# Turning x1's first half inside the attention loop, with its terms in DRAM, and attention and mixing in one block

## The chip, the cores and the metric

The kernel runs on one core of a Trainium2 chip. The metric is the device time of one execution in microseconds (us), taken as the median of several runs; the kernel before needs 1972.02 us (three runs, 1969.37 to 1972.77). The names of the engines are those of the profile: PE (matmuls; PEld is its weight load), DVE (vector), ACT (scalar activation), POOL (GpSimd), and SP, which in this kernel issues every DMA, in the order in which its program is written.

## The reference

Two residual layers run over x (2048 rows by 1024 columns, float32). The first is gated linear attention, the second a causal pooling mixer. What is computed, cut to what matters here:

```python
# layer 0: gated linear attention, chunks of 64 rows
q, k, v, g, lr = split(x @ gla_w_in)
o = o_intra + qe @ S_prev                       # o_intra: masked scores @ v
o = o * rsqrt(mean(o**2) + 1e-6) * norm_w * silu(g)
x1 = layernorm(4**0.25 * x + o @ gla_w_out)
# layer 1: pooling mixer
u, z = split(x1 @ pool_w_in)                    # 2048 columns each
p = causal_window_means(u) - u                  # windows of 2, 4, 8, 16 rows
m = (p @ w_grp + b_grp) * scale
out = layernorm(4**0.25 * x1 + (m * silu(z)) @ pool_w_out)
```

## The kernel before

Every large float32 product is split: an operand is written as a high part (a rounded copy, made by ACT) and a low part (the operand minus the high part, made by DVE), and `split_product` (L198) issues three matmuls, high by high, low by high, high by low. The large products are further done by a seven-product scheme on 2 by 2 blocks (`PRODUCTS`, `ORDER` = 1, 5, 6, 2, 7, 3, 4), so that each "step" of the projection and mixing stages is seven products of four k slices each, and the operand x has seven terms: blocks 1, 2 and 3 are quarters of x itself, terms 5, 6, 7 and 4 are sums and differences of quarters.

The program runs in four stages, one block each: `prepare` (fuses pooling weights with the group weights), `project` (x @ gla_w_in), `attend_and_norm` (attention, output projection and layer norm, giving x1), and `pool_mix_and_out` (the mixing stage and the final projection). At the end of a block every engine waits for all others.

**Attention** takes 16 tiles of 128 rows. In step t, PE does the scores and the state update of tile t, then the first half of the output projection of tile t - 2 (`y_half`, with the two matmuls of `mean` for tile t - 1 in the middle), then `outputs` of tile t, then the second half of the projection. ACT and DVE make the high and low parts, the gate, and the norm of tile t - 3; SP loads q, k, k2, kn, v for tile t + 2, g, and x, and stores x1's tile t - 3. Steps 4 to 13 are a hardware loop, the others are written out.

**Mixing** has 32 steps (16 pairs of weight columns, over x1's first half and then its second half), and 16 output steps. x1 is needed transposed. Its second half is turned on the way, during steps 2 to 9, in eight "chunks": `load_stage_rows` brings rows of x1 back from DRAM, PE transposes them (`turn_stage`), ACT copies them out of PSUM (`copy_stage`), POOL makes the four sums (`stage_terms`), and SP stores seven pieces into the DRAM scratch `x_terms` (`store_stage`). When the operand set changes (after step 15, `LAST_OF_EPOCH`), the terms are loaded from there; ACT and DVE split them (`turn_hi`, `turn_lo`), except that in the first step after a change the products at positions 4 and 5 (`NATIVE`; terms 7 and 3) run unsplit on the raw term (L2250), so that their splitting can come later. The first half has no such step before it: at the start of the mixing block it is turned at once. `turn_first` transposes 4 times 2 row tiles, `first_parts` and `first_terms` (ACT), `first_term` (POOL) and `first_sums`, `first_terms_lo` (DVE) make all terms with their high and low parts, and only then can step 0's first product start.

## Time and profile before

| what | us |
|---|---|
| median of the runs | 1972.02 (1969.37 to 1972.77) |
| the profiled execution, whole | 1964.6 |
| its span, first to last instruction | 1962.9 |
| PE busy | 1861.6 (95%) |
| DVE busy | 1398.3 (71%) |
| ACT busy | 852.5 (43%) |
| POOL busy | 598.2 (30%) |

The profile is of one execution. A row of a timeline gives the start, the duration, the engine, the line of the kernel and the tiles written and read; what stands in brackets is how long the engine was idle before it and what ended that. The recorded duration of a matmul is longer than its share of a pipelined row: the distance from one start to the next is what a matmul costs there. The slices of the page show PE at 9 tenths nearly everywhere, with two dips, one near 640 us (the border between projection and attention) and one near 970 us (the border between attention and mixing).

### The profile page before, as it was taken

To read this page: it belongs to the slowest core of one execution; us is meant where nothing else is said; L and a number is where in the kernel's file an instruction comes from. 1 tells how busy PE (TensorE), PEld (TensorE's weight loads), DVE (VectorE), ACT (ScalarE), POOL (GpSimd) and SP (SyncE) were. 2 spreads that over 40 slices of the span, in tenths; PEclk is the share of its full clock that TensorE was granted. 3 is DMA by queue.
4 is the path that set the end of the run, shared out by engine and by line. 5 is a ranking of instruction groups with operands and counts; after the bars stand their busy time and mean duration, and the time that the engine had idled before them with its cause. 6 is when DMAs were issued, how large, how long until landed. Compare 5 with 4: busy or idle time off the path is not lost.

```text
span 1962.9 us, 24653 instructions
## 1 busy us (share of the span) xinstructions
PE 1861.6 (95%) x8688; PEld 1535.0 (78%) x8688; DVE 1398.3 (71%) x1769; ACT 852.5 (43%) x1323; POOL 598.2 (30%) x380
## 2 busy tenths in 40 slices
PE   8989999999999699999679999999999998999997
PEld 7878887886788588888558888887888786887786
DVE  3454555778667678787666788768899967546997
ACT  4554445657555434333444444344333344224221
POOL 1322231332221000000145665405566532323330
PEclk9999999999999799999879999999999999999999
DMA  8967572557365645443413544242546326556442
GB/s 286 321 200 266 195 248 97 152 141 247 90 171 179 239 145 188 171 162 138 171 43 116 170 150 144 98 172 75 178 170 221 140 93 215 208 192 257 161 151 97
DMA packets 259725, 336.43 MB, mean 171 GB/s; under 512 B 18208, under 2 KB 187936, under 8 KB 255904
## 3 DMA queue, kind: packets, MB, share of 16 engines
q1 hardware_dynamic: 259616, 335.02, 50.9%
q8 instruction: 63, 1.03, 0.2%
q14 instruction: 46, 0.38, 0.1%
HBM read 218.58 MB, written 116.39 MB: 171 GB/s over the span
## 4 chain that ended last, share of the span: by engine, by line
PE 38%; DVE 7%; issue 4%; ACT 1%; POOL 0%; DVEq 0%; ACTq 0%; POOLq 0%
PE banks L200 13%; PE banks L202 12%; PE banks L201 12%; DVE m_w_lo L2520 2%; DVE m_x_lo L2534 1%; DVE m_win_a L2550 1%; ACT m_x_hi L2310 0%; DVE m_res L2633 0%; DVE m_win_b L2550 0%; DVE m_x_lo L2512 0%; PE banks L2203 0%; PE banks L2250 0%; DVE m_win_b L2566 0%; DVE m_res L2617 0%; DVE m_x_lo L2494 0%
## 5 line engine op out<-in xcount | busy, mean ns | idle before, releaser
L200 PE MATMUL banks<-m_x_hi,m_w_hi 128*128 128x512 f32 x1320 | 517.7, 392 | 12.6 <-DVE m_z L2596 6.6
L201 PE MATMUL banks<-m_x_lo,m_w_hi 128*128 128x512 f32 x1320 | 515.1, 390 | 0.0
L202 PE MATMUL banks<-m_x_hi,m_w_lo 128*128 128x512 f32 x1320 | 514.9, 390 | 0.0
L200 PEld LDWEIGHTS banks<-m_x_hi,m_w_hi 128*128 128x128 f32 x1320 | 248.8, 188 | 68.7 <-DVE m_w_lo L2520 10.6
L202 PEld LDWEIGHTS banks<-m_x_hi,m_w_lo 128*128 128x128 f32 x1320 | 248.7, 188 | 52.1
L201 PEld LDWEIGHTS banks<-m_x_lo,m_w_hi 128*128 128x128 f32 x1320 | 248.6, 188 | 51.8 <-issue 0.7
L200 PE MATMUL banks<-b_hi,h_w_hi 128*128 128x512 f32 x656 | 257.9, 393 | 6.1 <-issue 4.5
L202 PE MATMUL banks<-b_hi,h_w_lo 128*128 128x512 f32 x656 | 256.3, 391 | 0.0
L201 PE MATMUL banks<-b_lo,h_w_hi 128*128 128x512 f32 x656 | 256.0, 390 | 0.0
L2298 ACT ACTIVATE m_w_hi<-m_s 128x512 fp32r<-128x512 f32 x184 | 115.5, 629 | 186.2 <-PE banks L202 166.0
L2436 POOL TENSOR_TENSOR m_s<-pair_raw 128x512 f32<-128x512 f32 x24 | 46.7, 1945 | 469.0 <-POOLq L1512 365.1
L2520 DVE TENSOR_TENSOR m_w_lo<-m_s,m_w_hi 128x512 fp32r<-128x512 f32 x184 | 157.5, 857 | 32.3 <-ACT m_w_hi L2298 30.2
L200 PEld LDWEIGHTS banks<-b_hi,h_w_hi 128*128 128x128 f32 x656 | 123.6, 188 | 33.8 <-issue 8.6
L202 PEld LDWEIGHTS banks<-b_hi,h_w_lo 128*128 128x128 f32 x656 | 123.5, 188 | 26.0
L201 PEld LDWEIGHTS banks<-b_lo,h_w_hi 128*128 128x128 f32 x656 | 123.7, 189 | 25.4
L1224 DVE TENSOR_TENSOR h_w_lo<-h_s,h_w_hi 128x512 fp32r<-128x512 f32 x94 | 70.3, 753 | 48.9 <-ACT h_w_hi L954 48.3
L200 PE MATMUL banks<-a_w_hi,a_o_hi 128*128 128x512 f32 x256 | 101.5, 397 | 2.3 <-DVE a_res L1748 1.7
L201 PE MATMUL banks<-a_w_lo,a_o_hi 128*128 128x512 f32 x256 | 100.1, 391 | 0.0
L202 PE MATMUL banks<-a_w_hi,a_o_lo 128*128 128x512 f32 x256 | 100.0, 390 | 0.0
L2520 DVE TENSOR_TENSOR m_w_lo<-m_pair_raw,m_w_hi 128x512 fp32r<-128x512 f32 x69 | 65.2, 945 | 44.7 <-ACT m_w_hi L2298 44.1
L2520 DVE TENSOR_TENSOR m_w_lo<-pair_raw,m_w_hi 128x512 fp32r<-128x512 f32 x72 | 61.4, 853 | 43.5 <-ACT m_w_hi L2298 42.7
L2441 POOL TENSOR_TENSOR m_s<-pair_raw 128x512 f32<-128x512 f32 x24 | 43.4, 1807 | 133.3 <-PE banks L2250 86.0
(276 smaller groups left out, 3363.2 us busy)
## 6 DMA issues: line engine op xcount, KB each, us to landing
b_raw<-x_in SPq DMA_DIRECT2D x14, 1024.0 KB, 9.8
p_in<-in_pool_w_in SPq DMA_DIRECT2D x32, 256.0 KB, 5.7
w_fused<-p_out SPq DMA_DIRECT2D x32, 256.0 KB, 3.5
x_in<-h_terms SPq DMA_DIRECT2D x8, 1024.0 KB, 4.3
v_tiles<-h_v_out SPq DMA_DIRECT2D x16, 512.0 KB, 4.0
in_raw<-in_gla_w_in SPq DMA_DIRECT2D x16, 512.0 KB, 5.3
h_raw<-in_gla_w_in SPq DMA_DIRECT2D x16, 512.0 KB, 5.9
k<-k_tiles SPq DMA_DIRECT2D x32, 256.0 KB, 4.2
```

The costliest lines, as they stand in the source:

```text
L200: nc.tensor.matmul(out, a_hi, b_hi, start=first, stop=False, skip_group_check=True)
L201: nc.tensor.matmul(out, a_hi, b_lo, start=False, stop=False, skip_group_check=True)
L202: return nc.tensor.matmul(out, a_lo, b_hi, start=False, stop=last, skip_group_check=True)
L1224: nc.vector.tensor_tensor(w_lo[j][:], weights(i, j), w_hi[j][:].bitcast(F32), ALU.subtract).then_inc(w_lo_done, 1)
L2298: nc.scalar.activation(w_hi[ORDER[n]][:], weights(s, ORDER[n]), ACT.Copy).then_inc(w_hi_done, 1)
L2436: nc.gpsimd.tensor_tensor(s1[:], a21, a22, ALU.add).then_inc(w_summed, 1)
L2441: nc.gpsimd.tensor_tensor(s3[:], a11, a21, ALU.subtract).then_inc(w_summed, 1)
L2520: nc.vector.tensor_tensor(w_lo[j][:], weights(s, j), w_hi[j][:].bitcast(F32), ALU.subtract).then_inc(w_lo_done, 1)
L2534: nc.vector.tensor_tensor(x_lo[j][:], (ahead[n] if n < PRELOADED else x_raw[j])[:], x_hi[j][:].bitcast(F32), ALU.subtract).then_inc(x_lo_d ...
L2550: nc.vector.tensor_tensor(dst[:, first:PAD + HALF], src[:, first:PAD + HALF], src[:, first - step:PAD + HALF - step], ALU.add).then_inc(ch ...
```

## The change

Every line number of this section and of its order rows with "after" is of the changed kernel. x1's first half is treated as its second half already was. `x_terms` gets a second set. In attention steps 8 to 15, chunk c = t - 8 of the first half is turned: SP loads two pieces of rows (128 by 2 by 256 each, two buffers), PE transposes the first after `outputs` and the second after the second `y_half`, both into the PSUM bank that `mean` uses; ACT copies each out; POOL makes the sums; one step later SP stores seven pieces. Steps 8 to 17 are now written out, and only 4 to 7 stay in the hardware loop. Attention and mixing become one block: there is no point between them where all engines meet. The last tile's residual, norm and store move into the beginning of the mixing stage (`last_residual`, `last_rstd`, `last_shift`, `last_scale`, `last_end`, `store_last`). Terms 1, 5 and 6 of the first half are loaded while attention's last two steps run (`load_first`), terms 2, 7 and 4 after attention's last matmul (`y_ended`), term 3 after x1's last tile is stored. In step 0, products at positions 4 and 5 run unsplit. Before attention, the last four stores of g, the loads of ln_g and ln_b and half of gla_w_out move from the end of the projection block into the attention block.

```diff
-    ROWS, ROWS_PREFETCHED = 4, 4
+    ROWS = 2
...
-        self.x_terms = scratch("x_terms", [PRODUCTS, P, KT // 2, BLK])
+        self.x_terms = scratch("x_terms", [2, PRODUCTS, P, KT // 2, BLK])
...
                     if i == STEPS - 1 and n >= 1:
                         sp.wait_ge(product_mm, PRODUCTS * i + n + 1)
-                        if n == 1:
-                            p.load_norm(sp)
-                        for o in {2: (0,), 3: (1, 2), 4: (3,)}.get(n, ()):
-                            p.load_out_rows(sp, o)
+                        if n in (2, 3):
+                            p.load_out_rows(sp, n - 2)
             store_kn(LAST)
-            store_gates(LAST)
...
+    STAGED = NT // 2
+    CHUNKS = NT // 2
...
+        def load_stage_rows(c, pair, kk, r):
+            if c:
+                sp.wait_ge(st_turned, c * 2 - 1 + r)
+            sp.wait_ge(out_stored[kk], (pair - 1) * DMA)
+            sp.wait_ge(out_stored[1 - kk], (pair + (kk - 2)) * DMA)
+            rows = p.x1[ds((pair + 4 * r - STAGED // 2) * P, P), :].rearrange("p (h c) -> p h c", h=2)
+            sp.dma_start(stage_rows[r][:], rows[:, :, kk * 2 * P:(kk + 1) * 2 * P]).then_inc(st_rows[r], DMA)
+        def store_stage(c, pair, kk):
+            sp.wait_ge(st_sum, c * 4)
+            cols = ds((pair + (-STAGED // 2 if kk else -STAGED // 2 - 1)) * P, P)
+            k = (1 - kk) * 2
+            for j, src in ((1, stage_a[:, 0, :, :]), (2, stage_a[:, 1, :, :]), (3, stage_b[:, 1, :, :]),
+                           (5, stage_t[:, 0, :, :]), (6, stage_t[:, 1, :, :]), (7, stage_t[:, 2, :, :]),
+                           (4, stage_t[:, 3, :, :])):
+                sp.dma_start(p.x_terms[0, j - 1, :, k:k + 2, cols], src).then_inc(st_stored, DMA)
+        for i in range(4):
+            first, col = (2 + i % 2) * HALF_K, (HEADS - 1) * 2 + i // 2
+            sp.dma_start(p.g_tiles[first:first + HALF_K, :, col * P:(col + 1) * P].rearrange("t p c -> p t c"),
+                         p.g_main[:, i, :].rearrange("p (t c) -> p t c", c=P)).then_inc(p.g_stored[0], DMA)
         for s, n in enumerate((6 * 4, 2 * 4)):
             sp.wait_ge(p.g_stored[s], n * DMA)
         for stored, n in ((p.q_stored, 2), (p.k_stored, 4), (p.kn_stored, 2)):
             sp.wait_ge(stored, 2 * HEADS * n * DMA)
+        p.load_qkv(sp, 1, 1)
+        load_g(0, 0)
+        for n in (2, 3):
+            p.load_out_rows(sp, n)
+        load_g(1, 1)
+        load_x(0, 0)
+        p.load_norm(sp)
+        load_x(1, 1)
+        def step(t, s, lag, pair, c=None):
+            static = isinstance(t, int)
+            if staged(c):
+                for r in range(2):
+                    load_stage_rows(c, pair, s, r)
+            if static and t == NT:
+                sp.wait_ge(o_mm, NT)
+                sp.wait_ge(kv_mm, NT - 1)
+                p.load_pair(sp, p.pair_raw0, GT, 0)
+                store_stage(c, pair, s)
+                sp.wait_ge(st_stored, CHUNKS * PRODUCTS * DMA)
+                load_first(sp)
+            if lag >= 1 and not (static and t + 1 >= NT):
+                sp.wait_ge(gated_done, t)
+                load_g(t + 1, 1 - s)
+            if has(t, lag, TAIL):
+                sp.wait_ge(out_done, (t - TAIL) * 2 + 2)
+                sp.dma_start(p.x1[ds((t - TAIL) * P, P), :], out[1 - s][:]).then_inc(out_stored[1 - s], DMA)
+            if staged_before(c) and t < NT:
+                store_stage(c, pair, s)
+            if not (static and t + 2 >= NT):
+                sp.wait_ge(o_mm, t + 1)
+                p.load_qkv(sp, t + 2, s)
+            if lag >= LAG and not (static and t >= NT):
+                sp.wait_ge(y_read, (t - LAG) * 2 + 2)
+                load_x(t, s)
...
+            if staged_before(c):
+                pe.wait_ge(st_copied, c * 2)
...
+        def turn_stage(t, c, r):
+            pe.wait_ge(st_rows[r], (c + 1) * DMA)
+            if r:
+                pe.wait_ge(st_copied, c * 2 + 1)
+            else:
+                pe.wait_ge(rms_mid, t)
+            for b in range(4):
+                last = nc.tensor.transpose(sum_ps[:, b * P:(b + 1) * P], stage_rows[r][:, b // 2, b % 2 * P:(b % 2 + 1) * P],
+                                           p.ident[:])
+            last.then_inc(st_turned, 1)
...
+        def copy_stage(c, r):
+            act.wait_ge(st_turned, c * 2 + (r + 1))
+            if c:
+                act.wait_ge(st_sum, c * 4)
+                act.wait_ge(st_stored, c * (PRODUCTS * DMA))
+            stage = stage_b if r else stage_a
+            nc.scalar.activation(stage[:].rearrange("p h k t -> p (h k t)"), sum_ps, ACT.Copy).then_inc(st_copied, 1)
...
+    def gpsimd(pool):
+        t1, t2, t3, t4 = (stage_t[:, n, :, :] for n in range(4))
+        b11, b21, b12, b22 = stage_a[:, 0, :, :], stage_a[:, 1, :, :], stage_b[:, 0, :, :], stage_b[:, 1, :, :]
+        for c in range(CHUNKS):
+            pool.wait_ge(st_copied, 2 * c + 2)
+            if c:
+                pool.wait_ge(st_stored, c * PRODUCTS * DMA)
+            nc.gpsimd.tensor_tensor(t1, b12, b11, ALU.subtract).then_inc(st_sum, 1)
+            nc.gpsimd.tensor_tensor(t3, b22, b12, ALU.subtract).then_inc(st_sum, 1)
+            pool.wait_ge(st_sum, 4 * c + 1)
+            nc.gpsimd.tensor_tensor(t2, b22, t1, ALU.subtract).then_inc(st_sum, 1)
+            pool.wait_ge(st_sum, 4 * c + 3)
+            nc.gpsimd.tensor_tensor(t4, b21, t2, ALU.subtract).then_inc(st_sum, 1)
...
-    LAST_OF_EPOCH = (MT - 1, MIX - 1, SECOND - 1)
+    LAST_OF_EPOCH = (-1, MT - 1, MIX - 1, SECOND - 1)
...
+    def load_first(sp):
+        for n, dst in enumerate((ahead[0], ahead[1], first_raw)):
+            sp.dma_start(dst[:], p.x_terms[0, ORDER[n] - 1]).then_inc(x_loaded[n], DMA)
...
+        y_ended()
+        load_x(0, 3)
+        load_x(0, 4)
+        load_pair(1)
+        load_x(0, 6)
+        store_last()
+        load_x(0, 5)
...
+        for n in range(3):
+            hi_part(0, n)
+        for n in range(PRELOADED):
+            turn_hi(0, n)
+        y_ended()
+        turn_hi(0, 2)
+        hi_part(0, 3)
+        last_rstd()
         for i in range(STEPS):
...
+            if i == 0:
+                turn_hi(0, 3)
+                last_scale()
+                nc.scalar.preload_act_table_set("silu_and_others")
...
+        for n in range(3):
+            lo_part(0, n)
+        for n in range(PRELOADED):
+            turn_lo(0, n)
+        last_residual()
+        turn_lo(0, 2)
+        lo_part(0, 3)
+        last_shift()
...
+            if i == 0:
+                turn_lo(0, 3)
             next_lo(i, 0)
...
+            if i == 0:
+                last_end()
+                nc.vector.memset(h_in[:, 0:PAD], 0.0)
```

The first place is SP around the border between projection and attention. `g_tiles` and `kn_tiles` are scratches in DRAM, `a_w_raw` is gla_w_out, and the two branches are the end of one block and the start of the next. Before:

```order
L184 DMA a_w_raw<-in_gla_w_out 128x2x1024 x3
L732 DMA k_tiles<-h_e_k 128x4x128
L732 DMA k_tiles<-h_k_out 128x4x128
L732 DMA kn_tiles<-h_kn_out 128x4x128 x2
L732 DMA g_tiles<-h_g_main 128x4x128 x4
L673 UNCONDITIONAL_BRANCH
L1514 UNCONDITIONAL_BRANCH
L163 DMA q_97<-q_tiles 128x4x128
```

After:

```order
L726 DMA kn_tiles<-h_kn_out 128x4x128 x2
L667 UNCONDITIONAL_BRANCH
L2830 UNCONDITIONAL_BRANCH
L1551 DMA g_tiles<-h_g_main 128x4x128 x4
L168 DMA q_97<-q_tiles 128x4x128
L172 DMA k_98<-k_tiles 128x512
L172 DMA k_99<-k_tiles 128x512
L172 DMA kn_100<-kn_tiles 128x512
L172 DMA v_101<-v_tiles 128x1024
L1526 DMA a_g_7098<-g_tiles 128x1024
L184 DMA a_w_raw<-in_gla_w_out 128x2x1024 x2
```

The four stores of g moved behind the border, and two of the four loads of gla_w_out behind the loads of tile 1.

The second place is PE in an attention step, between `outputs` (`a_scores`, `a_state`) and the second half of the output projection (`a_w_hi`, `a_o_hi`). After:

```order
L1668 MATMUL banks<-q_87,a_state_7116 128x128 x4
L1663 MATMUL banks<-a_scores_7096,v_91 128x128 x4
L1668 MATMUL banks<-q_87,a_state_7116 128x128 x4
L1637 MATMUL banks<-ident,a_stage_rows_7130 128x128 x4
L193 MATMUL banks<-a_w_hi,a_o_hi_7112 128x512
```

Before, the row with `a_stage_rows` is not there; a second such row stands at the end of each of these steps.

The third place is the border between attention and mixing, on PE first. Before:

```order
L202 MATMUL banks<-a_w_hi,a_o_lo_7124 128x512
L1512 UNCONDITIONAL_BRANCH
L2175 UNCONDITIONAL_BRANCH
L2187 MATMUL banks<-ident,rows_102 128x128 x8
L2187 MATMUL banks<-ident,rows_103 128x128 x8
```

After, where m_x_hi and m_w_hi are the mixing stage's operands:

```order
L195 MATMUL banks<-a_w_hi,a_o_lo_7115 128x512
L2378 MATMUL banks<-m_x_hi_7163,m_w_hi_7157 128x512
L193 MATMUL banks<-m_x_hi_7163,m_w_hi_7157 128x512
```

and on SP there, from the last chunk's stores on, after:

```order
L1547 DMA x_terms<-m_stage_t 128x2x128 x4
L2151 DMA m_ahead_7192<-x_terms 128x2048
L2151 DMA m_ahead_7193<-x_terms 128x2048
L2151 DMA m_first_raw<-x_terms 128x2048
L1583 DMA x<-a_out_7125 128x1024
L1583 DMA x<-a_out_7124 128x1024
L2182 DMA m_x_raw_7140<-x_terms 128x2048
L2182 DMA m_x_raw_7143<-x_terms 128x2048
L177 DMA m_pair_raw_7156<-w_fused 128x1024
L178 DMA m_pair_raw_7156<-in_pool_w_in 128x8x128
L2182 DMA m_x_raw_7172<-x_terms 128x2048
L1595 DMA x<-a_out_7125 128x1024
```

The eight groups of transposes and the block's border left PE's program here; SP's loads of whole terms (128x2048, 1 MB each) took the place of the eight loads of rows.

## Rows read from the trace of the kernel before

**Rows 1.** The page, its part on busy time by engine.
```profile
PE 1861.6 (95%) x8688; PEld 1535.0 (78%) x8688; DVE 1398.3 (71%) x1769; ACT 852.5 (43%) x1323; POOL 598.2 (30%) x380
```

**Rows 2.** Windows: us, busy time of each engine, PEclk, DMA share, GB/s.
```profile
640.00:660.00 20.00, 11.28 (x72) 11.12 (x73) 9.49 (x17) 6.24 (x7) 0.00 (x0) 0.66 0.88 294
...
800.00:850.00 50.00, 50.00 (x299) 44.09 (x298) 39.40 (x67) 19.65 (x28) 0.00 (x0) 1.00 0.51 177
...
970.00:990.00 20.00, 8.31 (x48) 7.49 (x46) 19.68 (x29) 15.54 (x29) 6.98 (x6) 0.67 0.59 191
990.00:1000.00 10.00, 1.50 (x4) 1.24 (x5) 9.90 (x15) 7.40 (x13) 4.77 (x4) 0.50 0.05 15
```

**Rows 3.** Waits of PE from 960 us on: total us, times, longest.
```profile
PE banks L2245 <- DVE m_x_lo L2503: 14.3, 1, 14.3
PE banks L2187 <- PEq L1512: 7.1, 1, 7.1
```

**Rows 4.** Timeline of PE, opening of the mixing stage: start us, us, instruction.
```profile
958.77 0.39 PE L202 MATMUL banks<-a_w_hi,a_o_lo 128*128 128x512 f32 x1
...
1019.87 0.39 PE L2245 MATMUL banks<-m_x_hi,m_w_hi 128*128 128x512 f32 x1
1020.10 0.39 PE L200 MATMUL banks<-m_x_hi,m_w_hi 128*128 128x512 f32 x1
1020.78 0.39 PE L200 MATMUL banks<-m_x_hi,m_w_hi 128*128 128x512 f32 x1
```

**Rows 5.** Timeline of PE, two unsplit products where the operand set changes.
```profile
1323.83 7.03 PE L2250 MATMUL banks<-m_x_raw,m_s 128*128 128x512 f32 x16
1330.30 0.79 PE L200 MATMUL banks<-m_x_hi,m_w_hi 128*128 128x512 f32 x1
```

**Rows 6.** Tile m_x_raw: ns min/median/max of an operation; DMA to landing.
```profile
L2310 ACT ACTIVATE m_x_hi<-m_x_raw x15: 1895/1903/1918, 1309.0 to 1812.3; 128x2048 fp32r<-128x2048 f32 x15
L2534 DVE TENSOR_TENSOR m_x_lo<-m_x_raw,m_x_hi x15: 2284/2293/3442, 1310.9 to 1818.5; 128x2048 fp32r<-128x2048 f32 x15
...
DMA to landing us min/median/max: 4.8/5.6/10.2
```

**Rows 7.** Timeline of SP, then of ACT: projection's last stores, first attention tiles.
```profile
638.83 3.59 SPq L732 DMA_DIRECT2D kn_tiles<-h_kn_out  x2
642.46 5.25 SPq L732 DMA_DIRECT2D g_tiles<-h_g_main  x4
651.23 0.57 SPq L163 DMA_DIRECT2D q<-q_tiles  x1
...
654.20 0.43 SPq L167 DMA_DIRECT2D v<-v_tiles  x1
...
658.63 0.63 ACT L1648 ACTIVATE a_kn_hi<-kn 128x512 fp32r<-128x512 f32 x1 [5.59 <-DMA v<-v_tiles]
```

**Rows 8.** Timeline of PE, then DVE: one tile of the attention loop.
```profile
842.54 0.33 PE L1589 MATMUL banks<-q,k 128*128 128x64 f32 x2
...
853.50 1.06 PE L1607 MATMUL banks<-a_scores,v 128*128 128x128 f32 x8
854.40 1.06 PE L1612 MATMUL banks<-q,a_state 128*128 128x128 f32 x8
...
860.75 0.33 PE L1589 MATMUL banks<-q,k 128*128 128x64 f32 x2
...
853.42 1.22 DVE L1737 TENSOR_TENSOR a_out<-a_out,a_ln_b 128x1024 f32<-128x1024 f32 x1
```

**Rows 9.** Tile m_stage_t: POOL's longest operation; DMA to landing.
```profile
L2454 POOL TENSOR_TENSOR m_stage_t<-m_stage_b x8: 1730/1736/1736, 1061.9 to 1201.8; 128x256 f32<-128x256 f32 x8
...
DMA to landing us min/median/max: 1.9/2.0/3.8
```

**Rows 10.** Timeline of SP: the seven stores of one chunk of terms.
```profile
1065.65 0.88 SPq L2049 DMA_DIRECT2D x_terms<-m_stage_a  x2
...
1067.12 2.12 SPq L2049 DMA_DIRECT2D x_terms<-m_stage_t  x4
```

More of the change, by code:

```diff
@@ L1491, in attend_and_norm, with run @@
     LAG, TAIL = 2, 3
-    def run(engine, step):
+    STAGED = NT // 2
+    CHUNKS = NT // 2
+    def run(engine, step, end):
         for t in range(TAIL + 1):
             step(t, t % 2, min(t, TAIL), t // 2)
-        with engine.Fori((TAIL + 1) // 2, NT // 2 - 1) as pair:
+        with engine.Fori((TAIL + 1) // 2, STAGED // 2) as pair:
             for s in range(2):
                 step(pair * 2 + s, s, TAIL, pair)
-        for t in range(NT - 2, NT + TAIL):
-            step(t, t % 2, TAIL, t // 2)
+        for t in range(STAGED, end):
+            step(t, t % 2, TAIL, t // 2, t - STAGED)
     def has(t, lag, behind):
@@ L1870, in pool_mix_and_out @@
     p.at = shared_at
-    first_a = [p.place(f"m_first_a{s}", [P, KT, P]) for s in range(2)]
-    first_b = [p.place(f"m_first_b{s}", [P, HALF_K, P]) for s in range(2)]
+    first_raw = p.place("m_first_raw", [P, HALF_K, BLK])
     p.at = shared_at
@@ L1876, in pool_mix_and_out @@
     assert p.at <= p.mix_raw_at
[L1877 to L1881 removed]
+    rows, rows_loaded = p.rows, p.rows_loaded
+    stage_a, stage_b, stage_t = p.stage_a, p.stage_b, p.stage_t
     p.at = p.rows_at
@@ L1931, in turns_to, with loaded @@
     def turns_to(e, n):
-        return PRODUCTS * (e - 1) + TURNS.index(n) + 1
+        return PRODUCTS * e + TURNS.index(n) + 1
+    def loaded(e, n):
+        if n < PRELOADED:
+            return ahead[n][:]
+        return first_raw[:] if (e, n) == (0, 2) else x_raw[ORDER[n]][:]
     def turning(turned, i, slot):
-        return [(epoch(i - later) + 1, n) for n, (later, at) in turned.items() if at == slot and follows(i - later)]
+        return [(LAST_OF_EPOCH.index(i - later), n) for n, (later, at) in turned.items()
+                if at == slot and i - later > 0 and follows(i - later)]
     def epoch(i):
-        return sum(i > last for last in LAST_OF_EPOCH)
+        return sum(i > last for last in LAST_OF_EPOCH) - 1
     def group(i):
```

1839 lines of the change are left out of this document (903 added, 936 removed).

## Prediction

> **What bounds the kernel now.** I read the busy times of the page first: PE is busy 95% of the span and the next engine 71% [rows 1], so time is either PE's work or the few holes in it. The slices show two holes, and a table of windows sizes them [rows 2]: in the attention loop PE is busy for all of 50 us at a granted clock of 1.00, while from 970 to 1000 it is busy 9.8 of 30 us, at 0.67 and then 0.50, with DVE busy 29.6 of the same 30 us. From 640 to 660 it is busy 11.3 of 20 us at 0.66, with the DMA engines at 0.88. The waits of PE then name what ends the holes of the mixing stage's opening [rows 3]: 7.1 us at the block's border and 14.3 us for DVE's low parts of the first half of x1. The opening is therefore bound by DVE, the attention loop by PE, the border at 640 by SP and the DMA queue. A change counts where it touches one of these.
>
> **The opening, removed part.** Attention's last matmul starts at 958.77, so at the pitch of 0.23 us PE is free at about 959.1; the marker matmul that begins step 1 starts at 1019.87 [rows 4]. The opening with step 0 costs 60.8 us now. A step without a stall is seven products of 4 triples, and a triple takes 0.68 us (1020.10 to 1020.78) [rows 4]: 7 x 2.72 = 19.0 us. So 41.8 us of the 60.8 are hole, transposes and the lower clock.
>
> **The opening, what takes its place.** Five split products take 13.6 us; two unsplit ones take 1330.30 - 1323.83 = 6.5 us [rows 5], so step 0 is 20.1 us of PE work. What is late next are operands. I count from 959.1 as 0.
> - Terms 1 and 5 are loaded during the last two attention steps. Chunk 7 is copied at about -22 (the start of step 16 plus 3 us), its sums take up to 4 x 1.74 = 7 us [rows 9], its stores 3.6 us of issue and 2.0 to land [rows 9, 10]: SP issues the loads at about -10. A load of 1 MB lands in 5.6 us [rows 6], and three in a row follow each other every 3 us (294 GB/s at a share of 0.88 [rows 2] is 334 GB/s of a full queue): -4.5, -1.5, +1.5. ACT needs 1.9 and DVE 2.3 us for a term [rows 6]: low parts at -0.4 and +2.4. Products 0 and 1 start without a wait to speak of and end at +5.7.
> - Term 6: DVE does the last tile's residual first (two additions and two statistics over 512 columns, half the width of an operation of 1.22 us [rows 8], so 2.5 us, and the aggregate; I take 3.2), then 2.3 us: low part at about +8. Stall 2 us, product 2 ends at +10.5.
> - Term 2 is issued at +0.1 only, lands at +5.7, but ACT is held by the seed copy and the last norm's scale, so its high part comes at +9 and its low part at +11.5. Stall 1 us, product 3 ends at +14.2, the unsplit product 4 at +17.5.
> - Term 3 is loaded behind x1's last tile. DVE's last two operations of 1.22 us [rows 8] end at about +15, SP issues store and load until +15.7, the load lands 5.6 us later, plus 1 us for the 0.5 MB store ahead of it: +22. Stall 4.5 us, product 5 ends at +25.5, product 6 at +28.
> So step 1 begins 28 us after attention's last matmul, not 60.8: the gain is 32.8, say 32. From both sides: if the two late places (terms 6 and 2, and term 3) cost nothing, 20.1 + 2 us, a gain of 38; if the loads take their longest 10.2 us in both serial places [rows 6], 2 x 4.6 us more and a few us at the lower clock, a gain of 21 at least.
>
> **The border at 640, moved part.** SP needs 3.6 us to issue two stores of kn and 5.25 us to issue four of g, and only then does the block end (PE and ACT start again at 648) [rows 7]. An issue of a free queue takes about 0.4 us [rows 10]: SP is held by the queue, into which 3 MB of gla_w_out and 1 MB for ln had just gone. After the change 2 MB + 1 MB of that come later and the border no longer waits for g, so the first attention tile starts about 7 us earlier. But the second tile waits for its own load, which waits for the stores of g: ACT waits 5.59 us for v, until 658.63, issued at 654.20 [rows 7]. That load can now be issued when g has landed: g issued 641 to 643, landed by 646.5 instead of 651, v landed by 654. I take 4 us of gain, with 0 (the new loads of 4 MB queue ahead of tile 2's) and 7 (the whole shift) as ends. PE idles longer before tile 1, and the clock there is already at 0.66 [rows 2].
>
> **The attention loop, added part.** Eight steps get 8 transposes each. The nearest rows are groups of eight 128x128 matmuls, 0.90 us from one to the next [rows 8]; PE has no free time there [rows 2], so 8 x 0.90 = 7.2 us, 0.3 to 0.5 less because PE waits anyway at the start of step 16. The same 64 transposes leave the opening, where they lay in the hole and are in the 60.8 us. ACT's two copies and SP's two loads and seven stores lie beside PE's work: ACT is busy 19.65 of 50 us [rows 2].
> The wait that is added is the one to look at. PE's second turn of chunk c waits for ACT's first copy of it, and that copy waits until the seven stores of chunk c - 1 have landed (buffers m_stage are single). Behind the turn stand the next tile's scores; behind ACT's copy the norm's rstd and then sum_hi, for which `mean` waits. In a step that starts at 842.54 (0): SP is free for the stores when x1's tile is, 854.64 plus 0.4, so 12.5; the stores are issued until 16.1 and the last lands at 17.6 to 18.1 [rows 8 to 10]; ACT's copy ends at 18.2 to 18.7. PE ends the second half of y at 18.2 now (860.75) [rows 8] and at 18.65 with the first four transposes. The chain closes within about 0 us, on either side. With a landing of 3.8 us, the longest of the stage rows [rows 9], it is late by 1.8 us, seven times: 12 us. I take 0.6 us a step, 4 us in all.
> POOL's four sums now run beside DVE, where POOL was idle (0.00 in the loop) [rows 2]. That DVE can be held is seen elsewhere: the same low part takes 2.29 us in the median and 3.44 at the longest [rows 6], so up to 1.15 us an operation.
> The Trainium skill ("SBUF — State Buffer", Who interferes with whom) says that a DVE instruction with two SBUF inputs and a GpSimd one that reads SBUF share a read interface, and the later one blocks for the whole of the other. By that rule the product with g and the two norm operations (both inputs in SBUF) can each stand behind a sum, and x1's tile would be done later; no row of the loop can show it, since POOL is idle there.
>
> **The sum.** 1964.6 (the profiled execution, 1.7 more than its span) - 32 - 4 + 7 + 4 = 1939.6, that is 25 us less. The median of the runs stands 7.4 us above the profiled execution; the same difference gives 1972.0 - 25 = 1947.
>
> **The rivals.**
> - A: everything closes (opening gain 38, border 7, no stall in the loop): -38 - 7 + 7 = -38, 1934. For it: PE's waits in today's operand changes are short, rows 5 show none. Against it: term 3's load hangs on the last tile's store, and nothing lies between.
> - B: the loads are the new bound of the opening. They land in about 10 us, PE's holes of 7 to 9 us bring the lower clock with them (0.67 in a comparable stretch [rows 2]), the gain is 21, and the border gives nothing because tile 2's load queues behind the moved 3 MB: -21 + 7 + 4 = -10, 1962. For it: the DMA queue is at 0.88 at the border. Against: at +0 in the opening little else is queued.
> - C, on the other side: the chain of the stage does not close in a step. x1's tile done, seven stores landed, ACT's copy, PE's second turn: whatever makes it late is paid seven times on PE. It decides from (32 + 4 - 7) / 7 = 4.1 us a step; three DVE operations held by 1.15 us each [rows 6] and a landing of 3.8 us [rows 9] make 3.5 + 1.8 = 5.3 us a step, 37 us in all, less 29: 8 us slower, 1980. The rule of the skill above would bring this case about. For it: the single buffer, and all links serial. Against: stage stores in the mixing stage land in 2.0 us, and POOL's sums end before DVE's norm operations begin, if they start 3 us into the step.
> - D: the opening's gain is given back in steps 1 and 2, because ACT and DVE owe the splitting of terms 4, 7 and 3 on top of the next weights. Then the gain shrinks to within the measurement, about 1970. Against: the same debt exists after steps 15 and 31, and PE has no wait there [rows 5].
>
> **How the numbers follow.** Forecast 0.60, A 0.15, B 0.15, C 0.05, D 0.05. Predicted 1947; the range from A to B, 1931 to 1962, leaves C, D and the far edges of A and B out. About 0.2% (4 us) is what a measurement of this kernel can tell from no change. Faster: forecast, A, B and a little of D, 0.91; same 0.04; slower 0.05.
>
> **What would show it.** PE between attention's last matmul and step 1's marker: 28 us, with three waits (2, 1, 4.5 us), the last for a DMA into m_x_raw. The waits of 14.3 us for DVE's low parts and of 7.1 us at the border are gone. Attention steps 8 to 15 are 19.1 us long plus at most 1, against 18.2. PE starts attention near 641 and tile 1 near 654. PE's span shrinks by 25 us though its work grows by 1 us. I am wrong if the attention steps grow by 3 us or more (C), or if a wait of over 8 us stands in step 0 (B).

## The result and the profile after

The changed kernel took 1959.21 us (median of 4 runs, 1954.36 to 1961.29) beside 1972.39 us (1969.37 to 1974.54) for the kernel before on the same chip: ratio 0.9931, interval 0.9908 to 0.9954, 13.2 us faster. Measured once more beside it, on another occasion, it took 1953.78 us against 1971.47: 0.9905 (0.9889 to 0.9922), 17.7 us. The forecast was 25 us, 1947. The direction and the place of the gain were right, its size was 0.5 to 0.7 of what was forecast. The two series of the same changed kernel lie 5.4 us apart (1954.36 to 1961.29, and 1950.05 to 1956.11). Below, medians of the experiments are compared with the second series, and a difference of a few us between two medians is not shown by them alone.

The profiled execution after has a span of 1952.6 us against 1962.9. Busy times of its page, beside [rows 1]: PE has 10 us more work in a span 10 us shorter, where the forecast had 1 us more.

```profile
PE 1872.0 (96%) x8680; PEld 1532.2 (78%) x8680; DVE 1394.8 (71%) x1738; ACT 851.1 (44%) x1308; POOL 617.6 (32%) x404
```

The same windows as [rows 2] (us, busy time and instructions of each engine, granted clock, DMA share, GB/s):

```profile
640.00:660.00 20.00, 13.36 (x78) 12.81 (x77) 11.93 (x20) 8.53 (x12) 0.00 (x0) 0.76 0.81 253
800.00:850.00 50.00, 49.93 (x309) 44.13 (x309) 37.55 (x64) 20.54 (x31) 7.70 (x11) 1.00 0.72 234
970.00:990.00 20.00, 15.70 (x60) 10.71 (x58) 16.04 (x19) 14.46 (x18) 4.19 (x3) 1.00 0.68 249
990.00:1000.00 10.00, 6.37 (x10) 2.90 (x11) 5.50 (x5) 2.43 (x2) 0.13 (x1) 0.66 0.53 186
```

The hole of [rows 2] at 970 to 1000 is mostly filled: PE is busy 22.1 of 30 us, against 9.8. What is left of it stands in the waits of PE from 950 to 1010 us (total, times, longest), beside [rows 3]:

```profile
PE banks L2383 <- issue: 5.9, 1, 5.9
PE banks L193 <- DVE a_res L1866: 4.7, 1, 4.7
PE banks L2383 <- ACT m_u L2491: 1.3, 1, 1.3
PE banks L193 <- issue: 0.7, 1, 0.7
```

The waits of 14.3 us for DVE's low parts and of 7.1 us at the border are gone, as forecast. The 5.9 us stand in step 0 at the unsplit product of term 3, whose load came late, as forecast with 4.5. The 4.7 us are new and were in no term: they stand in attention's tail, at 957.91.

Stage by stage, with the last matmul of one stage as zero for the next (projection's last matmul, the same code in both, stood at 637.0 before and at 639.2 after; over all fourteen profiles of this study it varies from 637.0 to 641.6 with no change to its code, so spans of single profiles carry that error):

| stretch | before | after | forecast |
|---|---|---|---|
| opening: attention's last matmul to step 1 | 60.8 | 32.0 | -32; measured -28.8 |
| border: tile 1 after projection's last matmul | 21.7 | 18.5 | -4; -3.2 |
| attention steps 8 to 15, each | 18.22 | 19.08 | +7 and +4; +7.0 together |
| attention's tail: tile 15's first score matmul to the last matmul (longest wait in it) | 43.4 (0.87) | 48.7 (4.70) | 0; +5.3 |
| mixing, a plain step | 19.04 | 19.20 | 0; +7.2 over all |

-28.8 - 3.2 + 7.0 + 5.3 + 7.2 = -12.5, and with the 2.2 us by which the projection ended late the 10.3 us between the spans.

### The profile page after: what moved, and what is told of

The parts are those of the page before. It is cut to its first block, busy times and chain, and to the rows that moved or that the text cites. A ratio compares the mean times of both kernels' runs of the same rounds, so it can differ in the third digit from the quotient of the medians.

```text
span 1952.6 us, 24512 instructions
## 1 busy us (share of the span) xinstructions
PE 1872.0 (96%) x8680; PEld 1532.2 (78%) x8680; DVE 1394.8 (71%) x1738; ACT 851.1 (44%) x1308; POOL 617.6 (32%) x404
## 4 chain that ended last, share of the span: by engine, by line
PE 53%; DVE 6%; issue 4%; ACT 1%; SPq 1%; DMA 1%; POOL 0%; DVEq 0%; ACTq 0%; POOLq 0%
PE banks L193 16%; PE banks L195 16%; PE banks L194 16%; DVE m_w_lo L2598 1%; PE banks L1668 1%; PE banks L1663 1%; PE banks L2383 1%; DVE m_x_lo L2612 1%; DVE m_win_a L2631 1%; PE banks L1647 1%; DMA v<-v_tiles 1%; PE banks L1645 1%; SPq L172 0%; DVE m_win_b L2631 0%; ACT m_x_hi L2420 0%
## 5 line engine op out<-in xcount | busy, mean ns | idle before, releaser
L2598 DVE TENSOR_TENSOR m_w_lo<-m_s,m_w_hi 128x512 fp32r<-128x512 f32 x182 | 151.3, 832 | 27.3 <-ACT m_w_hi L2407 25.1
L1817 POOL TENSOR_TENSOR m_stage_t<-m_stage_b,m_stage_a 128x256 f32<-128x256 f32 x8 | 6.1, 765 | 318.5 <-ACT m_stage_b L1754 318.5
L2550 POOL TENSOR_TENSOR m_s<-pair_raw 128x512 f32<-128x512 f32 x24 | 46.9, 1953 | 132.7 <-PE banks L2383 87.5
```

The source lines that it names most:

```text
L2550: nc.gpsimd.tensor_tensor(s3[:], a11, a21, ALU.subtract).then_inc(w_summed, 1)
L2598: nc.vector.tensor_tensor(w_lo[j][:], weights(s, j), w_hi[j][:].bitcast(F32), ALU.subtract).then_inc(w_lo_done, 1)
```

## The experiments

**Is the longer mixing step of the program or of the run?** Both kernels once more, without an edit.

> The kernel before, unchanged, profiled again. In the two profiles of the result the mixing steps between 1040 and 1620 us follow each other every 19.04 us in the kernel before and every 19.20 us in the changed one, and the projection stage, whose code is the same in both, ends at 638.5 and 640.7 us. Theory M (the difference of the steps belongs to the run or the chip): profiled again, the steps stand anywhere between 19.04 and 19.20 us, and the projection's end anywhere between 638.5 and 640.7. Rival P (it belongs to the program, by where its buffers lie): the steps are again 19.04 us, within 0.03. Time: the same as before by both.

> The changed kernel, unchanged, profiled again beside the kernel before on one chip. Theory M (the run or the chip): the steps between 1040 and 1620 us are as long as those of the kernel before profiled on the same chip, within 0.05 us, and the two spans are then some 17 us apart. Rival P (the program): again 0.16 us longer a step, 7 us over the whole mixing stage, and the spans some 10 to 13 us apart. Time: -13 us by P, -17 by M, against the kernel before.

Measured: 1971.50 against 1971.47 us (ratio 0.9999, 0.9987 to 1.0011), and 1953.78. The stores of the mixed rows end a step on SP; they follow each other in the plain steps every 19.0 us in both profiles of the kernel before, every 19.2 us in both of the changed one. Theory M fell on the steps, it is the program, though the time, 17.7 us under the kernel before, was what M had (-17) and not the rival's -13: the series differ by more than the steps. The projection's end moved from 637.0 to 640.9 in the kernel before: that is the run.

The timeline of PE shows where in a step the 0.16 us are. Start, duration, instruction, of the kernel before; the two rows are the first matmuls of triples four triples apart, one product:

```profile
1263.31 0.39 PE L200 MATMUL banks<-m_x_hi,m_w_hi 128*128 128x512 f32 x1
...
1266.03 0.39 PE L200 MATMUL banks<-m_x_hi,m_w_hi 128*128 128x512 f32 x1
```

And of the changed kernel: the first matmul of product 6, then of product 2, of its third and fourth triple, and of product 7:

```profile
1245.72 0.39 PE L193 MATMUL banks<-m_x_hi,m_w_hi 128*128 128x512 f32 x1
...
1248.52 0.40 PE L193 MATMUL banks<-m_x_hi,m_w_hi 128*128 128x512 f32 x1
...
1249.91 0.39 PE L193 MATMUL banks<-m_x_hi,m_w_hi 128*128 128x512 f32 x1
1250.59 0.39 PE L193 MATMUL banks<-m_x_hi,m_w_hi 128*128 128x512 f32 x1
1251.27 0.39 PE L193 MATMUL banks<-m_x_hi,m_w_hi 128*128 128x512 f32 x1
```

Before, a product takes 2.72 us, 226.7 ns a matmul, always. After, product 6 takes 2.80 us, 233.3 ns a matmul; the matmuls behind it fall back to 226.7 within product 2. Product 4 takes 2.76. 0.08 + 0.04 + 0.04 = 0.16 us. The other four products keep 2.72. What sets product 6 apart is where its tiles lie in SBUF. Modulo 2048 bytes of a partition, the length of a row of 512 numbers, x begins at 1152 and the weights at 1216 (product 6), 1216 and 192 (product 4); in all other split products of the projection and mixing stages of both kernels the two are the same number.

Product 4's 1024 bytes are not a steady cost. From its eleventh matmul on it is back at 226.7 ns, as product 2 is from its eighth. And attention's output projection, in both kernels, has its moving rows (`a_w_hi`) at 192 and its weights (`a_o_hi`) at 1216, 1024 apart too, and settles at 226.7 ns: these two matmuls of the changed kernel are four triples apart.

```profile
964.29 0.39 PE L193 MATMUL banks<-a_w_hi,a_o_hi 128*128 128x512 f32 x1
...
967.01 0.39 PE L193 MATMUL banks<-a_w_hi,a_o_hi 128*128 128x512 f32 x1
```

The weights of one k slice are 512 bytes long, so even where both tiles begin alike, the slices meet at distances of 0, 512, 1024 and 1536 bytes. So all matmuls at 226.7 ns here have distances that are multiples of 512, and whether 512 or 2048 is the length that counts was not tested.

**Same phase.** Edit of the changed kernel:

```
-    p.at = p.mix_at
-    for j in (3, 6, 2, 7):
+    p.at = p.mix_at + 1088
+    for j in (3, 4, 2, 7):
...
-    place_hi(4)
-    place_lo(4)
+    place_hi(6)
+    place_lo(6)
```

> The changed kernel with its mixing operands placed anew: in all seven products the moving terms of x and the weights that they meet now begin at the same place modulo 2048 bytes of a partition, as they did in the kernel before (the low block of operands begins 1088 bytes later, products 6 and 4 exchange the places of their x terms, and the small statistics tiles move to the end). Nothing else differs. In the profiles taken so far the starts of the split matmuls in a plain mixing step stand 226.7 ns apart in the kernel before, in every product; in the changed kernel 226.7 in products 1, 5, 7 and 3, but 233.3 in product 6 (weights 64 bytes off the phase of x), 229.5 in product 2 behind it and 230.5 in product 4 (1024 off). Theory (the phase between weights and moving rows in SBUF sets the distance): 226.7 everywhere, a plain step 19.04 us again in place of 19.20, and -7 us (5.5 to 8) on the changed kernel, 25 us under the kernel before. Rival V (the distance comes from which engine or DMA is at work beside the product, not from the places): product 6, the third of a step, keeps 233.3 ns, and the time stays that of the changed kernel.

Every product takes 2.72 us again (kernel with the same phase, PE, one product):

```profile
1248.36 0.39 PE L193 MATMUL banks<-m_x_hi,m_w_hi 128*128 128x512 f32 x1
...
1251.08 0.39 PE L193 MATMUL banks<-m_x_hi,m_w_hi 128*128 128x512 f32 x1
```

From the first stored mixed row to the last matmul it needs 915.7 us, against 922.0 in the repeated changed kernel, 6.3 us, but only 3.6 against the 919.3 of its first profile. Over all profiles this stretch is 915.3 to 915.7 us in the three kernels in one phase, 917.9 to 923.0 in the seven with product 6 at 64 bytes off, and 913.7 and 917.4 in the kernel before: the plain steps repeat to 0.01 us, while steps 17, 26 and 32 vary by 1.6 to 3.1 us from run to run. So the gain of 0.15 us a plain step is shown; over the stage the averages lie 4.4 us apart, and how much of 7 us is left is not settled closer. The median, 1951.42 (0.9905 of the kernel before, 0.9886 to 0.9925), is 2.4 below that of the changed kernel, whose ratio on its own occasion was 0.9905 as well: the medians do not show this gain. Where POOL is held as well (below) it is 3.8, within the intervals too. Rival V fell on the distances of the matmuls.

**192 bytes.** Only `p.at = p.mix_at + 192` in place of `p.at = p.mix_at`.

> The changed kernel with the low block of mixing operands (x terms of products 3, 6, 2, 7, weights of 2, 7, 3) 192 bytes later, so that product 6's weights are 128 bytes short of its x's phase modulo 2048 in place of 64 past it, both on multiples of 64 but apart by a multiple of 128. Theory W (what counts is whether the two agree modulo 128): product 6 goes to 226.7 ns between starts, product 2 behind it too, a step loses 0.12 us. Theory X (what counts is the phase modulo 2048, the length of one row of 512): product 6 keeps more than 229 ns. Product 4 keeps 230.5 by X, whose operands are 1024 apart as before; by W its 230.5 has another cause, and stays too.

Product 6, now 128 bytes off, takes 2.79 us: 232.9 ns a matmul. Theory W fell, a common multiple of 128 is not enough. Product 4, 1024 off as before, went from 230.5 to 227.0 ns, which neither theory has; it is at 226.7 from its second matmul on here and from its eleventh there, so what changed is how it starts, and why is open. One execution, 1961.6 us.

**The same fault in the kernel before.** `p.at += 64` between its x terms and its weights.

> The kernel before, with 64 bytes left free between the x terms and the weights of its mixing stage, so that all seven products have their weights 64 bytes off the phase of x, and nothing else. Theory (phase): all split matmuls of the mixing stage stand 233.3 ns apart in place of 226.7, a plain step takes 19.60 us in place of 19.04, and the kernel is 46 steps of 0.5 us slower, +24 us (20 to 27). Rival V (the work beside the product): no change, within 2 us.

1990.47 us against 1971.11: ratio 1.0103 (1.008 to 1.0125), 19.4 us slower. All products take 2.80 us, a plain step 19.6. That is just under the expected range of 20 to 27, 5 less than the expected 24; 3.3 of these 5 are PE's waits for DVE from step 1 on, which fell from 17.4 to 14.1 us, since a slower PE meets its operands later. Rival V, which had no change, fell. This is the strongest test, since one number of the kernel before was changed and nothing of the change under study is in it.

**POOL held.** The first pair's sums wait for attention's last low part:

```
+        pool.wait_ge(o_lo_done, NT)
         weight_sums(0)
```

> POOL's four sums of the first pair of weights are held until DVE has written attention's last o_lo. Theory (the two-input instructions of DVE and POOL's sums block each other): in the changed kernel's profile DVE's operations at 947.29, 949.10, 951.45 and 953.57 took 1.89, 2.32, 2.20 and 2.28 us beside POOL's sums; alone they take 1.22 each as in the loop, PE's wait of 4.70 us at 957.91 falls to 1.5 or less, the low-clock triples behind it go, and the kernel gains 5 us (4 to 6.5) on the changed one: 18 us under the kernel before. POOL's sums then stand beside other work of DVE, and the opening keeps its time. Rival Q (the wait at 957.91 is the tail's own order: nothing is left for PE between tile 15's outputs and its y half): DVE's operations get shorter, but PE's wait stays above 3 us and the gain is under 2 us. Rival R (the held sums come late): the first product from sums, at step 0's second place, waits for them, and the gain is given back.

The timeline of the changed kernel, POOL and DVE in attention's tail (POOL's first sum before it meets DVE takes 1.29 us, and DVE's product with one input in a bank 1.22):

```profile
946.80 1.29 POOL L2545 TENSOR_TENSOR m_s<-pair_raw 128x512 f32<-128x512 f32 x1 [1.13 <-DMA pair_raw<-in_pool_w_in]
948.17 2.16 POOL L2548 TENSOR_TENSOR m_s<-m_s,pair_raw 128x512 f32<-128x512 f32 x1
950.29 2.27 POOL L2550 TENSOR_TENSOR m_s<-pair_raw 128x512 f32<-128x512 f32 x1
...
946.03 1.22 DVE L1842 TENSOR_TENSOR a_gated<-banks,a_rms 128x1024 f32<-128x1024 f32 x1 [2.55 <-ACT a_rms L1774]
947.29 1.89 DVE L1847 TENSOR_TENSOR a_gated<-a_gated,a_g 128x1024 f32<-128x1024 f32 x1
949.10 2.32 DVE L1853 TENSOR_TENSOR a_out<-a_out,a_ln_g 128x1024 f32<-128x1024 f32 x1
951.45 2.20 DVE L1855 TENSOR_TENSOR a_out<-a_out,a_ln_b 128x1024 f32<-128x1024 f32 x1
953.57 2.28 DVE L1935 TENSOR_TENSOR a_o_lo<-a_gated,a_o_hi 128x1024 fp32r<-128x1024 f32 x1
955.77 0.67 DVE L1866 SCALAR_TENSOR_TENSOR a_res<-a_x,banks 128x512 f32<-128x512 f32 x1
...
957.91 0.77 PE L193 MATMUL banks<-a_w_hi,a_o_hi 128*128 128x512 f32 x1 [4.70 <-DVE a_res L1866]
```

With POOL held:

```profile
946.02 1.22 DVE L1848 TENSOR_TENSOR a_gated<-a_gated,a_g 128x1024 f32<-128x1024 f32 x1
947.16 1.22 DVE L1854 TENSOR_TENSOR a_out<-a_out,a_ln_g 128x1024 f32<-128x1024 f32 x1
948.42 1.23 DVE L1856 TENSOR_TENSOR a_out<-a_out,a_ln_b 128x1024 f32<-128x1024 f32 x1
949.56 1.22 DVE L1936 TENSOR_TENSOR a_o_lo<-a_gated,a_o_hi 128x1024 fp32r<-128x1024 f32 x1
950.70 0.68 DVE L1867 SCALAR_TENSOR_TENSOR a_res<-a_x,banks 128x512 f32<-128x512 f32 x1
...
952.84 0.47 PE L193 MATMUL banks<-a_w_hi,a_o_hi 128*128 128x512 f32 x1 [0.88 <-DVE a_res L1867]
```

Four operations with both inputs in SBUF are 1.22 us each in place of 1.89 to 2.32; the one that reads a bank was not touched. PE's wait falls from 4.70 to 0.88 us, and the kernel takes 1947.91 us (0.9881, 0.9864 to 0.9897): 5.9 less than the changed kernel, and its slowest run, 1948.82, is faster than all eight of the changed kernel. The tail takes 43.4 us in this profile and in the two below that hold POOL, as in the kernel before, and 47.6 to 50.1 in the eight that do not. Theory right, Q fell. POOL's sums now stand beside DVE's residual, with one input in a bank, and its statistics, with one input, and those keep their 0.67 to 0.70 us. R was no part of it, but the opening did give something back: step 0 ended 33.8 us after the first mixing matmul, 31.7 and 29.5 in the two profiles of the changed kernel, and PE waited 3.0 us for ACT, which stood 3.35 us behind the load of pair 1.

**Term 3 early.** `load_x(0, 5)` goes into `ahead[0]` behind pair 1, before `store_last`; product, high and low part read it there.

> Term 3 of x1's first half is loaded into the buffer that term 1 leaves free, before attention's last store, and its products and turns read it there. Theory (PE's wait of 5.93 us at 993.63 is for that load, which stood behind the last store of x1, and the low clock behind it follows from the wait): the wait goes to under 0.5 us, the eight unsplit records behind it take 3.3 us again instead of 5.6, and the kernel gains 8 us (6 to 9) on the changed one: 21 us under the kernel before. Rival S (the transfers of the opening are the bound: six terms, a pair and the store share the queues, and term 3 as term 4 land late wherever they are issued): term 6 or term 4 is then late in its place, and the gain is 0 to 3 us. Rival T (the last tile's chain DVE to store_last, which DVE meets late, is next): the first half's copy into the padded rows, or the windows, wait instead, and the gain is under 4 us.

1954.52 us (0.9907, 0.9888 to 0.9926): no gain in the medians. The theory's 8 us did not come. The wait of 5.9 us is gone, and two for DVE stand in its place, at the last product of step 0 and at that of step 1 (from PE's waits, 955 to 1030 us):

```profile
PE banks L193 <- DVE m_z L2680: 3.0, 2, 1.5
PE banks L2385 <- ACT m_u L2494: 0.9, 1, 0.9
```

Yet in the profile step 1 begins 24.6 us after the first mixing matmul, not 29.7 or 32.0 (the 27.3 in the expectation of the kernel with all three, below, counts one product too many), and step 2 begins 3.5 to 5.7 us earlier than in the two profiles of the changed kernel. So DVE takes back a part, not all. The rest of this run was slower in stretches that the edit does not touch: attention's tail 50.1 us, and 923.0 from the first mixed row on.

**Held and same phase, and all three.**

> The changed kernel with POOL's first sums held (as e2_pool_held) and the operands in one phase (as e8_same_phase). Alone the two took 5.9 and 2.4 us off the changed kernel's median of 1953.8 us, the second 6 us behind step 1 in its profile, with an opening 1 to 3 us longer by the run. Theory (both gains add, they lie in different stages): split matmuls 226.7 ns apart, no wait of PE over 1 us in the tail of attention, 1943 us (1940 to 1946), 28 us under the kernel before. Rival S (what the tail gains, the opening loses, since its loads take their time): the stretch from the first mixing matmul to step 1 grows by 4 us or more, and the time is 1946 us or over.

> The same with term 3's early load as well (as e3_term3_early). Alone it gave no time (1954.5 against 1953.8 us), although step 1 began 27.3 us after the first mixing matmul in place of 29.5 to 31.7: attention's tail before it and one wait of 1.5 us for add_u3 behind it took that back in the one profile. Theory T (term 3's load is what step 0 waits for at its end, and 3 us go with it, of which 1.5 come back in a wait for DVE): 1 to 3 us less than e13_held_and_phase, 1941 us. Rival S (the six loads of 1 MB are the bound, whatever their order): the same time as e13_held_and_phase, within 1 us, with another term late.

1944.07 us (0.9871, 0.9853 to 0.9889) and 1942.37 us (0.9849, 0.9832 to 0.9865). In the profile of the first both gains are there, a tail of 43.4 us and products of 2.72 us, and an opening of 30.9 us beside 32.0 and 29.7 in the changed kernel, so rival S fell; that they add in the time is within its range (1940 to 1946), but beside POOL held alone it is not clear of the intervals. The next rows are the first mixing matmul and the one that begins step 1, first of the kernel held and in one phase, then of the one with term 3 early as well:

```profile
965.17 0.39 PE L2379 MATMUL banks<-m_x_hi,m_w_hi 128*128 128x512 f32 x1
996.02 0.39 PE L2379 MATMUL banks<-m_x_hi,m_w_hi 128*128 128x512 f32 x1
...
966.56 0.39 PE L2381 MATMUL banks<-m_x_hi,m_w_hi 128*128 128x512 f32 x1
992.76 0.39 PE L2381 MATMUL banks<-m_x_hi,m_w_hi 128*128 128x512 f32 x1
```

With term 3 early, step 1 begins 26.2 us behind the first in place of 30.9, 4.7 earlier. A wait of 1.6 us for DVE at the end of step 1 takes a part back; step 2 begins 3.1 us earlier, and the last matmul still is 3.1 earlier, as theory T has it and rival S has not. In the medians it is 1.7 us, within the intervals; attention took 1.8 us longer in this profile. This last kernel is 29.2 us faster than the kernel before, and 11.4 faster than the changed one.

**Sums twice.** Four more sums on POOL for each chunk, ahead of the ones that are stored.

> The changed kernel, in which POOL makes the four sums of each staged chunk of the attention loop twice (four more instructions of 0.74 us for each of the eight chunks, about 3.0 us, behind the copies and ahead of the sums that are stored). Theory (the chain of a chunk is set by SP's order and not by POOL: in the changed kernel's profile the copies end at 924.6, the sums at 927.6, but SP stores them at 933.4, behind the store of x1 that waits for DVE, and the next chunk's first copy starts on the stores' landing at 939.0): the sums end at 930.6, still before the store, and the time does not move, within 2 us. Rival C as the prediction priced it (the chain of copies, sums and stores sets the step once it is some 3 to 4 us longer): PE waits 1 to 3 us in each of seven steps, and the kernel loses 8 to 20 us.

1954.30 us, no change in the median. But attention steps 8 to 15 take 19.4 us, not 19.1, and PE waits three times for ACT's copy, 2.0 us. POOL's last sum now ends beside DVE's norm operation (DVE, then POOL, of this kernel):

```profile
877.49 1.76 DVE L1859 TENSOR_TENSOR a_out<-a_out,a_ln_g 128x1024 f32<-128x1024 f32 x1
...
876.56 1.60 POOL L1828 TENSOR_TENSOR m_stage_t<-m_stage_a,m_stage_t 128x256 f32<-128x256 f32 x1
```

1.76 in place of 1.22, and 1.60 in place of 0.74. The added 3 us of POOL work do not hold the store: the sums end at 878.16, x1's tile later. The 0.3 us a step fit the meeting, which makes x1's tile and so the stage stores later; no run has the one without the other. My theory was right on the time and had left out the meeting.

**A quarter of the transposes.** `for b in range(1)` in place of `range(4)` in the added turns.

> The changed kernel with one transpose in four of those added to the attention loop (16 of 64; the other parts of x1's first-half terms are then not x1's, the copies, sums and stores are as before). Theory (attention's longer steps are the transposes alone, on PE): the distance of the x1 stores in steps 8 to 15, now 19.1 us against 18.2 in the kernel before, falls to 18.4 us (18.3 to 18.6), and the kernel gains 5 us (4 to 6). Rival Y (it is the copies, sums and stores beside them that lengthen the steps: their DMA traffic, or ACT's two copies): the steps stay above 18.9 us.

1954.36 us, no change, and the x1 stores of steps 9 to 15 lie 19.1 us apart as before (818.5 to 933.2 in six steps). PE's waits from 800 to 950 us:

```profile
PE banks L1637 <- ACT m_stage_a L1754: 3.9, 5, 1.3
PE banks L1611 <- DVE a_sum_lo L1916: 1.4, 2, 1.1
```

Only step 8, in which no copy waits for earlier stores yet, is shorter: 18.45 us, for 19.13 in the changed kernel. The theory fell: the transposes alone do not set the 19.1 us, and the steps stay above 18.9, as rival Y has it. Its causes, traffic or ACT's two copies, were not tested one by one; the timeline of the changed kernel shows a loop of waits over the engines that is as long as the step:

```profile
864.02 0.69 DVE L1866 SCALAR_TENSOR_TENSOR a_res<-a_x,banks 128x512 f32<-128x512 f32 x1 [2.81 <-PE banks L195]
...
868.36 1.24 ACT L1735 ACTIVATE a_out<-a_res,a_shift,a_rstd 128x1024 f32<-128x1024 f32 x1 [0.98 <-DVE a_shift L1897]
...
874.53 1.22 DVE L1855 TENSOR_TENSOR a_out<-a_out,a_ln_b 128x1024 f32<-128x1024 f32 x1
...
875.78 0.35 SPq L1583 DMA_DIRECT2D x<-a_out  x1
...
878.40 1.98 SPq L1547 DMA_DIRECT2D x_terms<-m_stage_t  x4
...
882.10 0.60 ACT L1754 ACTIVATE m_stage_a<-banks 128x512 f32<-128x512 f32 x1 [3.91 <-DMA x_terms<-m_stage_t]
...
882.89 0.60 PE L1637 MATMUL banks<-ident,a_stage_rows 128*128 128x128 f32 x4
```

From the end of y on PE (863.82) over the residual, the norm, x1's store, the stage stores behind it on SP and their landing to ACT's copy (ends 882.70) and PE's second turn at 882.89: 19.07 us, 0.19 us of it slack. PE's own work and this loop are equally long. Take work from PE, and the loop holds the step.

**The border undone.** The loads of the norm rows and output weights and the stores of the last gates back where the kernel before issued them.

> The changed kernel with the border's part undone: the norm rows, all four parts of the output weights and the last group's gates go through SP where the kernel before issued them, at the end of the projection, and the loads at attention's start lose them. Between the projection's last matmul and the first y matmul lie 44.2, 45.1 and 44.6 us in the three profiles of kernels with the old border, and 41.3 to 43.1, on average 42.2, in the six with the new one. Theory: the border gives 2.5 us, so here this stretch is 44.6 us (44 to 45.3) again, and the kernel is 2.5 us slower than the changed one. Rival B as the prediction had it (the loads are late by themselves, the border gives nothing): the stretch stays at 42 us, and so does the time.

1961.03 us (0.9947, 0.9931 to 0.9962): 7 us slower than the changed kernel in its second series, 2 in its first. The stretch from projection's last matmul to the first y matmul is 47.8 us, not 44.6, and 40.3 to 43.1 in all ten profiles with the new border. SP is held by its two stores of kn for 5.42 us, where it was 3.59 [rows 7] and 1.38 in the repeated changed kernel:

```profile
641.21 5.42 SPq L726 DMA_DIRECT2D kn_tiles<-h_kn_out  x2
```

So the border's part is worth 4.7 to 7.5 us in this profile and up to 7 in the medians, more than the 3.2 read between the two kernels, and rival B fell. Why the old border costs 3 us more inside the new kernel than in the old one stays open.

## Why the forecast was right, and where it was not

- **The opening**, -32: right. The holes were filled in the forecast order, five loads, a tile's residual in between, and term 3 last. -28.8 in the first profile, -31 in the second (step 1 two us earlier). The wait for term 3 was 5.9 us for 4.5, and the matmuls behind it ran at the lower clock (0.66 from 990 to 1000 us). The 2 us for term 6 did not come, the wait for term 2 was 0.7 where 1 was forecast, and one of 1.3 us, for ACT's copy of a bank, was in no term. With term 3 early, waits for DVE of 1.5 us in each of steps 0 and 1 stand in its place, and 3.1 us are left of it in the profiles of the last two kernels.
- **The border**, -4: the mechanism was right; the two kernels show -3.2 and the undone part 5 to 7.
- **The transposes**, +7, and **the stage chain**, +4: these were added, and should have been compared. "The chain closes within about 0 us, on either side" was exact: it closes with 0.2 us to spare. Both give the same 19.1 us step, and the quarter of transposes, with 3.9 us of waits for ACT's copy in place of PE's work, speaks for two bounds side by side. The sum was 4 us too dear here.
- **Rival C** was near and did not come: POOL's sums (867.46 to 870.46) end before DVE's norm operations (873.28), as its "against" had it. Made twice as long, they meet them, and the step grew by 0.3 us, not 4. The Trainium skill ("SBUF — State Buffer", Who interferes with whom) has a DVE instruction with two SBUF inputs contend with a GpSimd one that reads SBUF, and the one that issues later block for the whole of the other. The rows above agree with the blocking: 1.22 and 1.29 us alone, 2.2 to 2.3 for either beside the other, 0.2 to 0.3 less than the sum.
- **Rival D**, the debt of splitting in steps 1 and 2: its "against" misread [rows 5], which end with the first step behind the change. The step after that one has a wait of 2.8 us in the kernel before:

```profile
1352.71 0.47 PE L200 MATMUL banks<-m_x_hi,m_w_hi 128*128 128x512 f32 x1 [2.79 <-DVE m_z L2596]
```

In the changed kernel steps 1 and 2 have no wait, so D did not come; with term 3 early one wait of this kind stands in step 1, 1.5 us.
- **Rivals A and B**: A needed no stall in the opening, and 5.9 us stood there. B needed a wait of over 8 us in step 0 and a border that gives nothing; neither came, though the first median, 1959, lies nearer to B's 1962 than to the forecast's 1947, for the two reasons that follow.
- **What failed**: the rule was weighed only where the stage sums stand, and not at the first sums of the mixing weights, which the one block lets POOL start in attention's tail. There four DVE operations in a row were held, +5.3 us in the profile, 5.9 in the medians with POOL held.
- **What was missing**: "step 0 is 20.1 us of PE work" and all steps behind it were taken at the old pitch. The change placed the operands of the mixing stage anew, and their phase in SBUF cost 0.15 us a step, 7.2 us over 46 steps between the two profiles; placing them in phase gave 3.6 to 6.3 back in the profiles, and nothing that the medians show.

Forecast -25; without the 4 us of the chain -29; with the two that were missed, 5.3 and 7.2, and 4 less of opening and border, -12.5. Half of the forecast gain went to two terms that the sum put at nothing; the measured time lies in the stated range because the range was wide and the chain's 4 us erred the other way, and that part is luck.

## What to carry to other kernels

When two stages become one block, list for every engine which of its instructions may now run earlier, and beside whom: an idle engine set free early can cost more than its work. When buffers are placed anew, keep weights and moving rows of a matmul at the same offset modulo the row (here multiples of 512 bytes apart did as well), and compare the distance of matmul starts, to the nanosecond, in a stretch whose code has not changed. Two bounds on one loop are compared, not added.

## What the runs showed of the hardware

- The distance of fp32r matmuls of 128x512 in a steady stream was 226.7 ns with weights and moving rows at the same offset modulo 2048 bytes, 233.3 with the weights 64 bytes further and 232.9 with them 128 bytes short, at a granted clock of 1.00 in all. 1024 bytes off it settled at 226.7 too; the start of such a product cost up to 0.04 us.
- DVE's operation on two SBUF inputs and POOL's sum each took nearly as long as both together: 1.22 and 1.29 us alone, 2.20 to 2.32 and 2.16 to 2.27 side by side. With POOL held, DVE's operations with one input in a bank (0.67 and 0.68 us) and with one input in all (0.70) kept their time beside the sums.
- In one program, code that had not changed ended between 637.0 and 641.6 us after the start over fourteen profiles.
